# Rotary positions and frequencies loaded in their final layout, angle work ahead of the first weight row, and weight row 1 held for x tile 0

## Time and profile before

| | |
|---|---|
| median of 3 runs | 302.25 us (301.93 to 302.3) |
| the profiled execution | 301.75 us |
| its span, first to last instruction | 300.0 us |
| TensorE matmul busy | 292.4 us (97%), 1373 matmuls |
| VectorE / ScalarE / GpSimd busy | 81% / 57% / 6% |
| granted TensorE clock, mean | 0.996 |
| DMA | 55.45 MB, mean 185 GB/s |

### The profile page before, as it was taken

How to read it: one execution, slowest core, us unless ns; L and a number is a source line. 1 busy time by engine, 2 the same in 40 slices (tenths; PEclk the granted TensorE clock), 3 DMA queues, 4 the chain that set the end, 5 groups by cost and what they waited for, 6 DMA issues and landing times.

```text
span 300.0 us, 4026 instructions
## 1 busy us (share of the span) xinstructions
PE 292.4 (97%) x1373; PEld 243.3 (81%) x1373; DVE 242.4 (81%) x403; ACT 171.6 (57%) x242; POOL 19.1 (6%) x41
## 2 busy tenths in 40 slices
PE   7999999999999999999999999999999999999992
PEld 7788888788898888887888888888888888888881
DVE  1999999977879687988888888889897978787155
ACT  2898999969765897717170808080808080813123
POOL 5050100000021001300000000000000000000011
PEclk9999999999999999999999999999999999999998
DMA  7987836737867121392929292929291929030003
GB/s 235 364 289 266 263 119 251 218 131 264 298 190 227 53 92 70 95 329 90 331 82 336 79 343 69 346 66 352 63 363 47 367 54 366 25 120 0 0 0 140
DMA packets 37318, 55.45 MB, mean 185 GB/s; under 512 B 2950, under 2 KB 26554, under 8 KB 37306
## 3 DMA queue, kind: packets, MB, share of 16 engines
q1 hardware_dynamic: 37140, 55.13, 54.4%
q10 hardware_dynamic: 166, 0.17, 0.2%
HBM read 53.72 MB, written 1.57 MB: 184 GB/s over the span
## 4 chain that ended last, share of the span: by engine, by line
PE 94%; DMA 2%; DVE 1%; issue 1%; POOL 1%; ACT 0%; SPq 0%; POOLq 0%; DVEq 0%
PE acc L508 15%; PE acc L510 15%; PE acc L509 15%; PE aux L508 13%; PE aux L509 13%; PE aux L510 13%; DMA raw<-in_w_in 2%; PE aux L613 1%; PE acc L562 1%; PE acc L565 1%; PE acc L568 1%; PE aux L683 1%; DVE x_sb L1366 1%; PE aux L707 1%; PE aux L665 1%
## 5 line engine op out<-in xcount | busy, mean ns | idle before, releaser
L1137 DVE TENSOR_TENSOR w_lo<-raw,w_hi 128x2048 fp32r<-128x2048 f32 x47 | 105.6, 2286 | 14.5 <-ACT w_hi L877 14.4
L877 ACT CAST w_hi<-raw 128x2048 fp32r<-128x2048 f32 x47 | 87.9, 1908 | 4.4 <-DMA raw<-in_w_ffn_up 2.1
L508 PE MATMUL aux<-w_hi,aT_hi 128*128 128x512 f32 (+1 forms) x180 | 69.8, 388 | 0.0
L509 PE MATMUL aux<-w_lo,aT_hi 128*128 128x512 f32 (+1 forms) x180 | 69.7, 387 | 0.0
L510 PE MATMUL aux<-w_hi,aT_lo 128*128 128x512 f32 (+1 forms) x180 | 69.7, 387 | 0.0
L1432 DVE STREAM_TRANSPOSE reuse_c<-reuse_c 32x128 f32<-32x128 f32 x160 | 48.4, 303 | 2.4
L1080 ACT CAST pT_hi<-reuse_c 128x512 fp32r<-128x512 f32 x10 | 6.2, 621 | 72.9 <-DVE reuse_c L1432 72.9
L508 PE MATMUL acc<-w_hi,aT_hi 128*128 128x512 f32 x118 | 47.1, 399 | 0.0
L510 PE MATMUL acc<-w_hi,aT_lo 128*128 128x512 f32 x118 | 46.1, 390 | 0.0
L509 PE MATMUL acc<-w_lo,aT_hi 128*128 128x512 f32 x118 | 46.0, 390 | 0.0
L508 PEld LDWEIGHTS aux<-w_hi,aT_hi 128*128 128x128 f32 x180 | 33.8, 188 | 6.9
(11 more groups left out here) (203 smaller groups left out, 285.0 us busy)
## 6 DMA issues: line engine op xcount, KB each, us to landing
raw<-in_w_ffn_gate SPq DMA_DIRECT2D x22, 512.0 KB, 4.3
raw<-in_w_ffn_up SPq DMA_DIRECT2D x22, 512.0 KB, 5.4
raw<-in_w_ffn_down SPq DMA_DIRECT2D x22, 512.0 KB, 6.0
raw<-in_w_in SPq DMA_DIRECT2D x20, 512.0 KB, 4.8
raw<-in_w_out SPq DMA_DIRECT2D x8, 512.0 KB, 4.3
raw<-in_w_in SPq DMA_DIRECT2D x8, 256.0 KB, 6.2
x_sb<-in_x SPq DMA_DIRECT2D x2, 512.0 KB, 3.7
m_moves<-reuse_c SPq DMA_DIRECT2D x1, 512.0 KB, 2.7
```

What stands on the lines that cost most here:

```text
L508: nc.tensor.matmul(dst, left_hi[:, k, tok], right_hi, start=first, stop=False)
L509: nc.tensor.matmul(dst, left_hi[:, k, tok], right_lo, start=False, stop=False)
L877: nc.scalar.copy(w_hi[:, slot % RING, :], raw[:, slot % RAW, :]).then_inc(hi_ready, 1)
L1137: nc.vector.tensor_tensor(w_lo[:, slot % RING, :], raw[:, slot % RAW, :], w_hi[:, slot % RING, :].bitcast(f32), ALU.subtract).then_inc(lo_ ...
```

## The change

Four things:

1. The positions are loaded with one token to a partition (128 x 2 int32), and the frequencies with the same row on every partition (128 x 64), both still on the ACT queue, positions first. The three TensorE transposes and the three VectorE copies between them go; one cast from int32 stays.
2. The angle product and the number of turns (with its split) move from behind the eight rows to the head of VectorE's work; the gains are copied between the two halves of it.
3. The norm 1 gain is loaded by SP, between x tile 0 and x tile 1.
4. SP issues row 0 and then waits until x tile 0 has landed, before it issues row 1.

```diff
--- before.py
+++ after.py
@@ -162,11 +162,8 @@
 
         low_w = w_hi[:, RING - 1, 0:KC * P].rearrange("p (k r w n) -> p k r w n", k=KC, w=2, n=RANK)
         turns_hi = w_lo[:, RING - 2, 0:P]
-        pos_i = reuse_c[0:T, 0:P].bitcast(i32)
-        pos_rows = reuse_c[0:T, P:2 * P]
-        freq_row = reuse_c[0:1, 2 * P:2 * P + HALF]
-        freq_col = reuse_c[0:HALF, 3 * P:3 * P + 1]
-        freq = acc[:, 3, P:P + HALF]
+        pos_i = reuse_c[:, 0:T].bitcast(i32)
+        freq = reuse_c[:, P:P + HALF]
         warm = w_lo[:, RING - 1, 0:SEQ]
         gain_rows = reuse_d[:, 0:P]
         other_rows = reuse_d[:, P:2 * P]
@@ -219,11 +216,7 @@
         up_loaded = sem("up_loaded")
         pos_loaded = sem("pos_loaded")
         freq_loaded = sem("freq_loaded")
-        pos_cast = sem("pos_cast")
-        pos_in_psum = sem("pos_in_psum")
         pos_ready = sem("pos_ready")
-        freq_in_psum = sem("freq_in_psum")
-        freq_ready = sem("freq_ready")
         gain_f_loaded = sem("gain_f_loaded")
         raw_loaded = [sem(f"raw_loaded_{s}") for s in range(RAW)]
         out_stored = sem("out_stored")
@@ -334,7 +327,11 @@
 
             for t in range(T):
                 sp.dma_start(x_sb[:, t, :], x[0, t * P:(t + 1) * P, :]).then_inc(x_loaded[t], 16)
-            for n in range(KC):
+                if t == 0:
+                    sp.dma_start(gain_rows[0:KC, :], norm1_gain.rearrange("l (k p) -> (l k) p", p=P)).then_inc(norm1_loaded, 16)
+            load_first(0)
+            sp.wait_ge(x_loaded[0], 16)
+            for n in range(1, KC):
                 load_first(n)
 
             def load_unit(slot, parts):
@@ -541,16 +538,9 @@
             pe.wait_ge(norm1_loaded, 16)
             nc.tensor.transpose(acc[:, 3, NORM1_ROW:NORM1_ROW + KC], gain_rows[0:KC, :],
                                 ident[0:KC, 0:KC]).then_inc(gains_in_psum, 1)
-            pe.wait_ge(freq_loaded, 16)
-            nc.tensor.transpose(acc[0:HALF, 0, 0:1], freq_row, ident[0:1, 0:1]).then_inc(freq_in_psum, 1)
             warm_up(2)
             pe.wait_ge(x_loaded[1], 16)
             x_transposed(1, range(4))
-            pe.wait_ge(gains_ready, 1)
-            pe.wait_ge(freq_ready, 1)
-            nc.tensor.transpose(freq, freq_col.to_broadcast([HALF, P]), ident[0:HALF, 0:HALF]).then_inc(freq_in_psum, 1)
-            pe.wait_ge(pos_cast, 1)
-            nc.tensor.transpose(acc[:, 3, KC:KC + T], pos_rows, ident[0:T, 0:T]).then_inc(pos_in_psum, 1)
 
             def first_row(k):
 
@@ -863,9 +853,9 @@
                 act.wait_ge(act_seq, n_seq[0])
 
 
-            act.dma_start(gain_rows[0:KC, :], norm1_gain.rearrange("l (k p) -> (l k) p", p=P)).then_inc(norm1_loaded, 16)
-            act.dma_start(freq_row, inv_freq).then_inc(freq_loaded, 16)
-            act.dma_start(pos_i, positions.rearrange("b (t p) -> (b t) p", p=P)).then_inc(pos_loaded, 16)
+            with nc.allow_non_contiguous_dma("one position a partition"):
+                act.dma_start(pos_i, positions.rearrange("b (t p) -> p (b t)", p=P)).then_inc(pos_loaded, 16)
+            act.dma_start(freq, inv_freq.to_broadcast([P, HALF])).then_inc(freq_loaded, 16)
             nc.scalar.preload_act_table(ACT.Exp)
 
             def split_as(slot, fills, used=None):
@@ -1159,13 +1149,26 @@
                                         ALU.subtract).then_inc(first_lo_ready, 1)
 
             nc.vector.memset(warm.bitcast(f32), 0.0).then_inc(warm_built, 1)
+            def nearest_turns():
+                then(nc.vector.tensor_scalar(turns, ang, 1.0 / (2.0 * np.pi), MAGIC, ALU.mult, ALU.add))
+                then(nc.vector.tensor_scalar(turns, turns, -MAGIC, None, ALU.add))
+
+            def take_off(n, part):
+                then(nc.vector.scalar_tensor_tensor(out=ang, in0=n, scalar=-part, in1=ang, op0=ALU.mult, op1=ALU.add))
+
+            dve.wait_ge(pos_loaded, 16)
+            nc.vector.tensor_copy(pos_f[:, :], pos_i).then_inc(pos_ready, 1)
+            dve.wait_ge(pos_ready, 1)
+            dve.wait_ge(freq_loaded, 16)
+            for t in range(T):
+                last = nc.vector.tensor_scalar(ang[:, t * HALF:(t + 1) * HALF], freq, pos_f[:, t:t + 1], None, ALU.mult)
+            then(last)
+            nearest_turns()
             dve.wait_ge(gains_in_psum, 1)
             nc.vector.tensor_copy(gains[:, 0:KC], acc[:, 3, 0:KC]).then_inc(gains_ready, 1)
             dve.wait_ge(gains_ready, 1)
-            dve.wait_ge(freq_in_psum, 1)
-            nc.vector.tensor_copy(freq_col, acc[0:HALF, 0, 0:1]).then_inc(freq_ready, 1)
-            dve.wait_ge(pos_loaded, 16)
-            nc.vector.tensor_copy(pos_rows, pos_i).then_inc(pos_cast, 1)
+            then(nc.vector.tensor_copy(turns_hi, turns))
+            then(nc.vector.tensor_tensor(turns_lo, turns, turns_hi.bitcast(f32), ALU.subtract))
 
             split_first(0)
             take_xT((0,))
@@ -1173,23 +1176,6 @@
                 take_xT((n,))
                 split_first(n)
 
-            def nearest_turns():
-                then(nc.vector.tensor_scalar(turns, ang, 1.0 / (2.0 * np.pi), MAGIC, ALU.mult, ALU.add))
-                then(nc.vector.tensor_scalar(turns, turns, -MAGIC, None, ALU.add))
-
-            def take_off(n, part):
-                then(nc.vector.scalar_tensor_tensor(out=ang, in0=n, scalar=-part, in1=ang, op0=ALU.mult, op1=ALU.add))
-
-            dve.wait_ge(pos_in_psum, 1)
-            nc.vector.tensor_copy(pos_f[:, :], acc[:, 3, KC:KC + T]).then_inc(pos_ready, 1)
-            dve.wait_ge(freq_in_psum, 2)
-            dve.wait_ge(pos_ready, 1)
-            for t in range(T):
-                last = nc.vector.tensor_scalar(ang[:, t * HALF:(t + 1) * HALF], freq[:, :], pos_f[:, t:t + 1], None, ALU.mult)
-            then(last)
-            nearest_turns()
-            then(nc.vector.tensor_copy(turns_hi, turns))
-            then(nc.vector.tensor_tensor(turns_lo, turns, turns_hi.bitcast(f32), ALU.subtract))
             split(2)
             for part in two_pi_parts(5)[:2]:
                 take_off(turns_hi.bitcast(f32), part)
```

## The result

The change made the kernel slower: 303.62 us median (302.82 to 303.74, 6 runs) against 302.16 (301.66 to 302.39, 6 runs) for the kernel before; the ratio is 1.0046, 95% interval 1.0036 to 1.0056. I had forecast 302.3 and a range up to 302.9. The profiled execution took 303.31 us with a span of 301.6, 1.6 us more than the 300.0 of before.

The account below looks back on a forecast made before the run. TensorE was taken to bound the kernel, its start set by row 0's landing. Five terms of 0 plus 0.05 us for smaller pieces, added to the 302.25 us median, gave 302.3 us, range 301.4 to 302.9.

Parts of the forecast that it names:

- What bounds the kernel: Whole kernel: TensorE, 94% of the span; its first real matmul at 7.64 us waits for row 0's landing.
- Smaller pieces: Loads of positions and frequencies at the start: 384 small pieces cost 0.05 us, bounds 0 and 0.3.
- Angle work moved ahead of row 0: VectorE before row 0's cast: frequencies land at about 4.2, block ends at about 6.3, before row 0; cost 0.
- my second rival: Start of VectorE: frequencies land late, at about 5.7 behind x tile 1, delaying TensorE; 302.85 us, chance 0.1.
- term 0: SP queue, row 1 held until x tile 0 lands: row 0 lands no sooner, no engine runs dry; gain taken as 0.
- my first rival: Weight row 0's load: without rows 1 to 7 behind it, lands at 6.4, not 7.05; 0.7 us gained, 301.6, chance 0.24.
- What leaves 16.35 to 18.22: VectorE behind the eight rows: unit 2's split ends 0.8 us sooner, but TensorE was not waiting; gains slack only, 0 us.
- Five operations out: Start of TensorE and VectorE: removed transposes and copies mostly sit in the cover of row 0's landing; worth 0.
- the order of the SP queue: SP's first loads: norm gain behind x tile 0 delays the issues of tile 1 and row 0 harmlessly; 0.

Follow-up runs that it names:

- the one product: Kernel before plus hold, frequencies spread by one TensorE product instead of two transposes, a copy, two warm-ups: 301.81 us; held from row 2 301.94; without hold 302.07.

## Why the prediction was wrong

- **What bounds the kernel** was read rightly for a later start and wrongly for a sooner one. The 1.59 us at the first real matmul are the 1.6 us of the span; but none of the three traces that start ahead of 7.64 ends sooner than the kernel before.
- **Smaller pieces: this step failed.** I took 0.05 us, with 0.3 as the upper bound, from low_raw's 1,024 pieces. Measured, the changed kernel with neither load is 1.2 us faster than with both (302.45 against 303.62); that includes VectorE's wait. The load of low_raw was no near case. Its pieces come from different addresses, and stand in SP's own queue behind others. The frequencies' pieces all read one address (2.1 us by themselves), and the positions, with a quarter of low_raw's pieces, hold up x tile 0 by 1.0 us (5.1 against 4.1) and may cost 0.5 us of time. The Trainium skill's rule against a strided last dimension (DMA: Bandwidth & Descriptors, Rules for kernel authors), which I had set aside, points the right way: tile 0 landed at 5.1 with the positions' 256 pieces and at 4.6 with 128.
- **Angle work moved ahead of row 0: the landing failed, the length held.** The block is 1.76 us, where I had worked out 1.61 + 0.19. I had the frequencies at 4.2; they came at 6.8. I inferred the landing of 128 pieces from that of one piece in the same place of the queue. The sign that I had named for my second rival (chance 0.1, 302.85) came, a wait of VectorE for the frequencies beyond 5.1. Its reason did not: they were not held behind x tile 1, which landed after them, at 7.4, but ran behind the positions' pieces. And the time was larger, because the same packets also hold up tile 0, tile 1 and row 0, which neither the forecast nor that rival had: 1.05 us of the 1.59 are row 0's later landing, 0.56 the block in front of its cast. The Trainium skill (the same page, Queues, rings and completion order) has the engines take turns between queues; the trace agrees in that 368 packets of ACT's queue run in the stretch of tile 0, while the engines fall to a quarter of their rate (91 against 378 GB/s). What I drew from it, that the frequencies' turn comes only after tile 1, did not come out.
- **The hold: term 0 was right in time and wrong in reason.** Row 0 does land 0.9 us sooner, my first rival's mechanism. But TensorE's front work ends no sooner, and a start that did come sooner (with the one product) was lost again on unit 2 and on VectorE's chain. I had called unit 2's landing set by bytes, at 15.5; with the hold alone it came at 16.1. In the changed kernel the hold probably saves something, up to a microsecond.
- **What leaves 16.35 to 18.22: "slack only"** held for unit 2 and missed L613 at 52.97, where TensorE arrives with nothing to spare. It did not decide this result, but it caps what any earlier start can give.
- **Five operations out, and the order of the SP queue:** the first was not measured by itself, and no run speaks against its 0; the norm gain's place costs 0.2 us by the medians, with intervals that begin at 0 or below.

Open is why reading one address is so slow, and why single executions put tile 1 anywhere from 5.6 to 7.0 with the same program. Open, too, is what sets the moment at which TensorE's clock goes up (4.2 to 12.3 us). In the trace in which it went up last, TensorE had stood idle for 0.7 us in front of tile 0. In the one with the frequencies only it stood idle for 1.4 us there, and the clock went up at 5.0.

## What to carry to other kernels

Do not price a small load by its bytes. 33 KB here cost most of 1.5 us, because their 384 pieces shared the engines with the first tile that everybody waits for and 128 of them read the same 256 bytes; 128 pieces from as many rows cost nothing that the time shows. Before an earlier start is counted as a gain, look for the next point at which TensorE arrives just in time; at L613 it had less than 0.1 us. A single trace's start is weak evidence while TensorE's pace may still change: look at the step of equal matmuls before a late start is put down to a load. When work is moved into a wait, everything queued behind it on that engine now hangs on its inputs, so its inputs must land with room to spare.

## What the runs showed of the hardware that I had not expected

- 128 reads of the same 256 bytes brought the 16 engines from 393 GB/s down to 155 to 185 while they lasted; 128 reads of 256 bytes at different addresses left them at 371 to 387.
- A load is slowed by what stands behind it in its own queue: row 0 took 5.3 us with seven rows issued behind it, 4.4 us with the next row issued only at 4.2 us. Two more pairs repeat it: 5.3 and 4.4 with the norm gain on SP, 5.8 and 4.5 with the one product, and 4.8 with one row behind it. The exception is the first run with neither small load, with the hold: 5.6, in an execution whose tile 1 was late as well.
- The slow stretch at the start of the weight rows was not taken away by the hold, only moved: 256 and 376 GB/s from 5 to 7 and 7 to 9 us before, 336 and 218 with the hold alone.
- TensorE's clock stood at its lower level from the start until 4.2 to 12.3 us, as the step of equal transposes shows (213 ns, then 109, in the changed kernel); the granted clock of 1.00 that the windows print there is not a record.
